# Half-row transposes in four attentions, and two-part 256-column products between the two units' updates in a delta rule

## The reference

```python
def attend(q, k, v):
    s = jnp.einsum('bqhgd,bkhd->bhgqk', q, k).astype(jnp.float32)
    p = jax.nn.softmax(s, axis=-1).astype(v.dtype)
    return jnp.einsum('bhgqk,bkhd->bqhgd', p, v)
```

## Time and profile before

| what | us |
|---|---|
| median of 3 runs (2487.32 to 2491.92) | 2490.42 |
| the profiled execution | 2487.92 |
| its span, first to last instruction | 2486.1 |
| PE busy | 2385.2 (96%) |
| DVE busy | 1712.9 (69%) |
| ACT busy | 1062.8 (43%) |
| POOL busy | 380.5 (15%) |
| mean granted TensorE clock | 0.994 of full speed |

### The profile page before, as it was taken

The page is one execution under the profiler, slowest core; times in us unless marked ns, Lnnn a source line. Parts: engine busy times, 40 slices in busy tenths (PEclk is TensorE's granted clock), DMA queues, the critical chain, the costliest instruction groups (busy, mean ns, idle before and its releaser), DMA issues.

```text
span 2486.1 us, 45211 instructions
## 1 busy us (share of the span) xinstructions
PE 2385.2 (96%) x17410; PEld 1922.4 (77%) x17410; DVE 1712.9 (69%) x2826; ACT 1062.8 (43%) x1748; POOL 380.5 (15%) x350
## 2 busy tenths in 40 slices
PE   6999999998888999999999999989999999999998
PEld 4888888866776878888788888767888885678877
DVE  3877787666565787778887763687777324776666
ACT  4232224356444622322523222475556334656354
POOL 2000001022444200000100001101002711211052
PEclk9999999999999999999999999999999999999999
DMA  7655663210000365566465553315564222113311
GB/s 294 225 194 191 194 201 125 93 39 3 4 4 19 104 215 194 192 194 203 144 216 193 191 176 99 109 38 161 186 184 138 90 97 91 31 52 128 117 45 52
DMA packets 89012, 324.76 MB, mean 131 GB/s; under 512 B 9888, under 2 KB 11040, under 8 KB 88096
## 3 DMA queue, kind: packets, MB, share of 16 engines
q1 hardware_dynamic: 86768, 310.15, 38.3%
q0 software_dynamic: 2096, 12.55, 1.5%
HBM read 321.49 MB, written 1.18 MB: 130 GB/s over the span
## 4 chain that ended last, share of the span: by engine, by line
PE 83%; DVE 8%; issue 3%; ACT 3%; DMA 1%; DVEq 1%; POOLq 0%; POOL 0%; ACTq 0%; SPq 0%
PE bank L522 20%; PE bank L523 20%; PE bank L524 20%; PE bank L532 5%; PE bank L533 3%; PE bank L1519 1%; DVE row_statistics L1577 1%; PE bank L1548 1%; PE bank L1530 1%; DMA projections<-stream_k 1%; DVE weights_hi_lo L427 1%; DVE work L1602 1%; PE bank L2414 1%; PE bank L1969 1%; PE bank L531 1%
## 5 line engine op out<-in xcount | busy, mean ns | idle before, releaser
L422 ACT ACTIVATE weights_hi_lo<-weight_ring 128x1024 fp32r<-128x1024 f32 (+1 forms) x338 | 352.2, 1042 | 992.0 <-PE bank L524 933.9
L522 PE MATMUL bank<-input_hi,weights_hi_lo 128*128 128x512 f32 (+1 forms) x1688 | 643.2, 381 | 12.3 <-DVE input_lo L866 4.5
L427 DVE TENSOR_TENSOR weights_hi_lo<-weight_ring,weights_hi_lo 128x1024 fp32r<-128x1024 f32 (+1 forms) x333 | 403.4, 1211 | 351.4 <-ACT weights_hi_lo L422 349.8
L523 PE MATMUL bank<-input_lo,weights_hi_lo 128*128 128x512 f32 (+1 forms) x1688 | 639.8, 379 | 0.0
L524 PE MATMUL bank<-input_hi,weights_hi_lo 128*128 128x512 f32 (+1 forms) x1688 | 639.5, 379 | 0.0
L522 PEld LDWEIGHTS bank<-input_hi,weights_hi_lo 128*128 128x128 f32 x1688 | 318.8, 189 | 79.0 <-issue 16.0
L524 PEld LDWEIGHTS bank<-input_hi,weights_hi_lo 128*128 128x128 f32 x1688 | 318.8, 189 | 59.6
L523 PEld LDWEIGHTS bank<-input_lo,weights_hi_lo 128*128 128x128 f32 x1688 | 318.8, 189 | 59.3 <-issue 0.7
L806 POOL TENSOR_TENSOR work<-work 128x512 f32<-128x512 f32 (+1 forms) x48 | 68.4, 1426 | 1225.2 <-ACT work L691 1224.3
L598 DVE CUSTOM_DVE_ANT_0 work<-weight_ring,extra_tiles 128x1024 f32<-128x1024 f32 x176 | 224.5, 1275 | 35.8 <-issue 13.2
L522 PE MATMUL bank<-hidden_hi_lo,weights_hi_lo 128*128 128x512 f32 x632 | 246.8, 390 | 0.0
(11 more groups left out here) (598 smaller groups left out, 3725.2 us busy)
## 6 DMA issues: line engine op xcount, KB each, us to landing
weight_ring<-stream_k SPq DMA_DIRECT2D x481, 512.0 KB, 3.4
weight_ring<-stream_f SPq DMA_DIRECT2D x64, 448.0 KB, 3.4
weight_ring<-stream_f SPq DMA_DIRECT2D x32, 512.0 KB, 3.7
projections<-stream_k SPq DMA_DIRECT2D x14, 512.0 KB, 6.5
extra_tiles<-condrows POOLq DMA_DIRECT2D x3, 1024.0 KB, 8.2
constants<-consts POOLq DMA_DIRECT2D x1, 2112.5 KB, 8.3
residual_stream<-xin SPq DMA_DIRECT2D x1, 2048.0 KB, 10.4
work<-nabias POOLq DMA_DIRECT2D x1, 2048.0 KB, 9.3
```

The lines of the kernel that those rows point to most:

```text
L422: act.activation(split_place(place)[:, 0, 0:words], w[:, 0:words], ACT.Copy).then_inc(hi_ready, 1)
L427: eng.tensor_tensor(split_place(place)[:, 1, 0:words], ring[:, n % RING, 0:words], split_place(place)[:, 0, 0:words].bitcast(F32), ALU.sub ...
L522: pe.matmul(out, weights[:, 0, w], x_hi, start=first, stop=False)
L523: pe.matmul(out, weights[:, 0, w], x_lo, start=False, stop=False)
```

## The change

The attentions' transposes are cut on the row halves: each 128 x 128 transpose becomes two, of 64 partitions (queries) x 128 keys, with a 64 x 64 piece of the identity; the half of the queries chooses the bank (4+h), and both heads share a bank. `attention_turned` becomes one flat row of 64-column pieces, and ScalarE's copy puts the halves back together through a crossed output view (as L2545 already does). The value products read the same numbers from the new places.

```diff
-            return BIG[:, 16 + u % 2 * 2:18 + u % 2 * 2, :] if which == "odd" else WORK[:, 20 + u % 2 * 2:22 + u % 2 * 2, :]
+            two = BIG[:, 16 + u % 2 * 2:18 + u % 2 * 2, :] if which == "odd" else WORK[:, 20 + u % 2 * 2:22 + u % 2 * 2, :]
+            return two.rearrange("p b t -> p (b t)")
...
+                    nt = len(key_tiles(which, pairs[u][1]))
                     for b in range(2):
-                        for i in range(len(key_tiles(which, pairs[u][1]))):
-                            mm = pe.transpose(pb[4 + b][:, tok(i)], attention_probs(which, u)[:, b, tok(i)], C("ident"))
+                        for i in range(nt):
+                            o = slice((b * nt + i) * HD, (b * nt + i + 1) * HD)
+                            for h, half in enumerate(HALF):
+                                mm = pe.transpose(pb[4 + h][:, o], attention_probs(which, u)[half, b, tok(i)], C("ident")[half, half])
                     mm.then_inc(probs_turned, 1)
...
-                    act.activation(attention_turned(which, u)[:, :, 0:nk], banks[:, 4:6, 0:nk], ACT.Copy).then_inc(turned_copied, 1)
+                    act.activation(crossed(attention_turned(which, u)[:, 0:2 * nk]),
+                                   banks[:, 4:6, 0:nk].rearrange("p h (i c) -> p h i c", c=HD), ACT.Copy).then_inc(turned_copied, 1)
```

```diff
+            for cols in (ALL,) if part is None else (((0, TC), (TC, T))[part],):
+                c = slice(*cols)
+                mm = pe.matmul(pb[6 + j % 2][:, c], C("blk"), BONUS_KEYS[:, j, c], start=True, stop=True)
+            if part != 0:
+                mm.then_inc(bonus_summed, 1)
...
+            c = slice(*cols)
+            mm = pe.matmul(pb[7][:, c], S(weights, low.start, low.stop, j * P, P), BIG[low, ranks, c], start=True, stop=True)
+            if c.stop == T:
+                mm.then_inc(lora_ready, 1)
...
-                if g < 3 and li < 4:
+                if g < 3 and li == 3:
                     wkv_low_rank(pe, 2 * g + 2 + li % 2, li // 2)
-                if g == 3 and li in (1, 2):
-                    bonus_sum(pe, li - 1)
                 for u in range(2):
                     q = NLEV * g + 2 * li + u
                     pe.wait_ge(x_copied, q + 1)
                     pe.wait_ge(turned_copied_back, q + 1)
                     (update if li < LAST else turned_update)(u).then_inc(z_ready, 1)
+                    if g < 3 and li < 3:
+                        wkv_low_rank(pe, 2 * g + 2 + li % 2, li // 2, (LAT if u else CTX))
+                    if g == 3 and li in (1, 2):
+                        bonus_sum(pe, li - 1, u)
```

More of the change, by code:

```diff
@@ L1548, in attend_tensor @@
                             mm = pe.matmul(mix_bank(which, u)[HD * b:HD * b + HD, 0:P], attention_values(which, tile, ch),
-                                           attention_turned(which, u)[:, b, tok(i)], start=i == 0, stop=i == len(keys) - 1)
+                                           attention_turned(which, u)[:, tok(b * len(keys) + i)], start=i == 0,
+                                           stop=i == len(keys) - 1)
                     mm.then_inc(mixed, 1)
@@ L2314, in wkv_low_ranks, with wkv_low_rank @@
               .then_inc(lora_ready, 1)
-        def wkv_low_rank(pe, n, part):
+        def wkv_low_rank(pe, n, part, cols=ALL):
             low, j = slice(HD * (n // 4), HD * (n // 4) + HD), n % 4
@@ L2323, in wkv_low_rank @@
             weights, ranks = (("w2", WL), ("a2", AL))[part]
-            pe.matmul(pb[7][:, :], S(weights, low.start, low.stop, j * P, P), BIG[low, ranks, :], start=True, stop=True)\
-              .then_inc(lora_ready, 1)
+            c = slice(*cols)
+            mm = pe.matmul(pb[7][:, c], S(weights, low.start, low.stop, j * P, P), BIG[low, ranks, c], start=True, stop=True)
+            if c.stop == T:
+                mm.then_inc(lora_ready, 1)
         def wkv_start_tensor(pe, g):
```

3 lines of the change are left out of this document (1 added, 2 removed).

## The result

| | us |
|---|---|
| kernel before, median of 7 runs | 2490.36 (2487.32 to 2494.63) |
| changed kernel, median of 7 runs | 2498.44 (2495.77 to 2501.94) |
| ratio, with 95% interval | 1.0033 (1.0023 to 1.0042) |
| forecast | 2485.4 (range 2480 to 2492) |
| profiled execution: span | 2496.7, before 2486.1 |

The time lies 13 us above the forecast and outside the range. The nearest of the rivals is C, the clock, with 2495.6 us, to which 0.10 was given.

What follows compares the result with a forecast made beforehand. TensorE was taken as the main bound (83% of the span; VectorE 8%), with VectorE close in all attentions but MLA. Attentions -5.8 us and delta rule +0.8 gave -5.0, from 2490.42 to 2485.4 us; range 2480 to 2492.

Steps and rivals of the forecast that it cites:

- C: Rival: shorter transposes lengthen idles in even, odd and NA, the clock falls, 1.7 us each; six falls 2495.6 us; chance 0.10.
- The level: Delta rule, groups 0 and 1: low-rank halves behind the updates make a level 4.70 us instead of 4.59.
- The three levels of group 2: Delta rule, group 2: low-rank halves cost +0.2 us for the three levels, an estimate.
- MLA: MLA attention: TensorE sets the pace, so the transposes' 4.5 us saving counts, less changes of array part: -2.2 us.
- Sets of halves: Attentions' transposes: sets of 8, 12 and 16 halves take about 0.39, 0.53 and 0.66 us.
- its -0.8: NA attention: VectorE is busy 9.55 of 10 us, so only the ends count: -0.8 us.
- The change of array part: TensorE, all stages: switching array part between sets costs about 0.17 us of idle.
- the later sigmoid: Delta rule: low-rank result 1.5 us later, costed at nothing; if the cover at groups' starts is gone, 4.5 us at most.
- odd -1.0 us: Odd attention: shorter sets mostly lengthen waits for VectorE's scaling, except where large products run late: -1.0 us.
- main case: Whole kernel: attentions -5.8 us and delta rule +0.8 us make -5.0 us, 2485.4 us; chance 0.5.
- Even -1.8: Even attention: VectorE becomes the bound half-way, so 0.4 of the transposes' 4.5 us saving counts: -1.8 us.

Runs made afterwards that it cites:

- e1_att: Kernel before with the half-row transposes in all four attentions alone, delta rule as before: ratio 0.9998.
- f1_mla: Kernel before with half-row transposes in MLA alone: ratio 0.9989.
- e3_l2whole: Changed kernel with the low-rank product of level 2 (groups 0 to 2) whole again and ahead of the updates: ratio 1.0009, 2491.8 us.
- e4_keys_late: Changed kernel, but GpSimd waits for both units' rates before starting the next group's keys: ratio 1.0010.
- e2_delta: Kernel before with the delta-rule edit alone (low-rank and bonus halves behind the updates): ratio 1.0021, 2494.0 us.
- f2_att_fill: Kernel before with half-row transposes in all four attentions, plus unread products on constants in the even and odd attentions' waits: ratio 0.9983.
- h_odd: Kernel before with half-row transposes in the odd attention alone: ratio 1.0025, 2496.3 us.
- k1_even_mla: Kernel before with half-row transposes in the even attention and MLA, the rest as before: ratio 0.9989, 2485.8 us.

## Why the prediction was wrong

**What held.** The level: 4.68 us against 4.70, the four sets behind the transposes 0.62 or 0.63 us apart. The three levels of group 2: +0.2 us together, as forecast. MLA: -2.3 against -2.2, alone -2.7 in time. Sets of halves: 12 in 1667.47 to 1667.99 = 0.52 us (0.53 said), 16 in 556.91 to 557.56 = 0.65 in e1_att (0.66 said). In NA the sets only wait longer; its -0.8 did not come (+0.1).

```profile
1667.47 0.45 PEld L1534 LDWEIGHTS bank<-constants,projections 64*128 64x128 f32 x12 [1.14 <-DVE projections L1607]
1667.99 0.63 PEld L1552 LDWEIGHTS bank<-projections 128*64 128x64 f32 x12
```

In MLA one price was wrong and another, just as wrong, made up for it. The change of array part was put at 0.17 us everywhere. Ahead of MLA's sets of 8, behind scores of 512 columns, TensorE now idles 0.76 us; but the sets of 4 that stood there had not held it 0.59 us either, as the earlier trace rows has it, but 0.96. The kernel before, then f1_mla, from the last of the scores' weight loads to the value products:

```profile
2125.34 0.19 PEld L1519 LDWEIGHTS bank<-extra_tiles,work 128*128 128x128 f32 x1 [0.24 <-issue]
2125.77 0.14 PEld L1530 LDWEIGHTS bank<-constants,work 128*128 128x128 f32 x1 [0.24 <-issue]
2126.20 0.36 PEld L1530 LDWEIGHTS bank<-constants,work 128*128 128x128 f32 x3 [0.29 <-issue]
2126.73 0.42 PEld L1548 LDWEIGHTS bank<-work 128*64 128x64 f32 x8 [0.17 <-issue]
```

```profile
2126.74 0.19 PEld L1520 LDWEIGHTS bank<-extra_tiles,work 128*128 128x128 f32 x1 [0.24 <-issue]
2127.69 0.33 PEld L1537 LDWEIGHTS bank<-constants,work 64*128 64x128 f32 x8 [0.76 <-issue]
2128.09 0.42 PEld L1555 LDWEIGHTS bank<-work 128*64 128x64 f32 x8
```

The pair wins 1.39 - 1.35 = 0.04 us, where the sum had 0.20 - 0.17 = 0.03. That it fits is luck.

**Step that failed: the later sigmoid, "I cost it at nothing", under "ScalarE, VectorE and GpSimd behind them".** The sigmoid's delay was seen and given one cover, GpSimd's wait at a group's start. What runs beside it was not looked at: GpSimd's keys meet VectorE's L2697 at level 3, and the level goes from 4.98 to 5.96 us in group 0, by 0.95 and 0.94 in the two others, +2.9 us. e3_l2whole and e4_keys_late, two different edits, both take it away, and bring the time from 1.0033 to 1.0009 and 1.0010. Behind it TensorE idles 1.85 us in place of 0.88, and the stretch of level 4 and the next group's start grows by 1.5, 0.6 and 1.7 us in the profile. Part of that is the clock (granted clock 0.74 in 612 to 618), but it differs between executions: the first of the three stretches took 28.66 us in the changed kernel, 26.32 in e2_delta with the same idle, and 26.25 to 28.74 in the profiles whose level 3 is as before. So the 2.9 us are shown, and how much the clock adds behind them is not.

**Step that failed: odd -1.0 us in the main case, and 0.10 for C.** The halves in the odd attention cost 6 us alone. C's mechanism was right: a longer idle, then half clock. f2_att_fill, with work in those waits, has the falls gone and 3.2 us less in the odd attention and behind it, up to MLA's first scores. Its chance was wrong. Three falls in some forty steps were read as rare, although showed one just where the change was to lengthen an idle of 2.54 us. It also looked at the stretch of the attention only; much of the price falls behind it, where dense products start at half clock (2.5 us up to MLA's first scores in h_odd, against 0.6 in the attention itself). That C's figure, 2495.6 us, came nearest to the 2498.4 measured is in part luck: it charged the clock with everything, and at least 2.9 us are GpSimd's and VectorE's overlap, which no rival had.

**Even -1.8.** Its size stays open: -0.8 in the profile, which is less than executions differ there, and -3.5 us in time alone (0.9986, which allows 1.0 to 5.7 us).

**What stays open.** The ratios of e1_att and e2_delta make 1.0019 together, the changed kernel has 1.0033; the intervals leave open whether the two edits add up. Which idle ends in a fall is not settled either: MLA's opening idles 2.29 us in the kernel before, without a fall, and in the changed kernel, with one. That fall stood in all eight profiles with halves in the odd attention and nothing added at MLA's opening, and in one of the eleven without such halves, k1_even_mla. So the odd attention's halves, over 400 us earlier, go with it, as h_odd's expectation had it, but they are not its only cause, and no run shows how the one would act on the other.

## What to carry to other kernels

When TensorE is made faster in a stage where another engine ends its waits, price the longer idle too: here the clock fell behind some of them, and the dense work that came next paid. Put only those stages on the new form in which TensorE sets the pace, and price each alone. When a result comes later, list what its consumers will then run beside, on VectorE and GpSimd above all, not only what they make wait.

## What the runs showed of the hardware

- VectorE's subtraction of two SBUF tiles (128 x 512) took 0.69 us when it began with GpSimd idle and 1.58 us when it began during a GpSimd instruction, ending 0.55 us after that one. GpSimd's L2617 took 1.28 us, and 1.52 when it began during such a subtraction.
- Eight transposes of 64 x 128 pieces on both row halves held TensorE 0.39 us, 12 took 0.52 and 16 took 0.65, against 0.81 and 1.02 for 6 and 8 full ones.
- Ahead of a weight load for another array part TensorE idled 0.76 us behind a product of 512 columns and 0.33 us behind one of 256.
- Seven products on constants, 1.64 us long in a wait of 2.29 us, went with a granted clock of 1.00 where the kernel without them had 0.72; by place 3.4 us were won, by the ratios 0.10%, which the intervals don't tell from nothing.
